# Expert weights of the third pair requested ahead of the first row gather, in a one-core encoder layer with a mixture of experts

## The reference, cut to what matters

```python
x = x + concat(A_out, B_out) @ w_out
h = rmsnorm(x, g_ffn)
# top-1 of 4 groups, then top-2 of the 8 experts inside the group
for e in range(32):
    gu  = h @ w_e_in[e]                        # 1024 x 512: gate | up
    act = silu(gu[:, :256]) * gu[:, 256:]
    out += gates[:, e:e+1] * (act @ w_e_out[e])   # 256 x 1024
y = rmsnorm(x + out, g_final)
```

## Time and profile before

| what | value |
|---|---|
| median of 3 runs | 601.9 us (601.87 to 603.3) |
| the profiled execution, its own time | 601.35 us |
| its span, first to last instruction | 599.6 us |
| mean granted TensorE clock | 0.972 |
| busy: PE, DVE, ACT, POOL | 545.6, 290.4, 166.0, 113.5 us |
| DMA queue q1 (SyncE): packets, MB | 39687, 139.63 |
| DMA queue q0 (GpSimd): packets, MB | 4464, 8.80 |

### The profile page before, as it was taken

How to read it: one execution, slowest core, us unless ns; L and a number is a source line. 1 busy time by engine, 2 the same in 40 slices (tenths; PEclk the granted TensorE clock), 3 DMA queues, 4 the chain that set the end, 5 groups by cost and what they waited for, 6 DMA issues and landing times.

```text
span 599.6 us, 7835 instructions
## 1 busy us (share of the span) xinstructions
PE 545.6 (91%) x3097; PEld 332.0 (55%) x3098; DVE 290.4 (48%) x496; ACT 166.0 (28%) x263; POOL 113.5 (19%) x181
## 2 busy tenths in 40 slices
PE   6999999999999898899999799999999778878993
PEld 5679999999765543444554674344443333333331
DVE  2862899998867546564455851211112110011147
ACT  4512123222766774652101111011010000000013
POOL 3100000312444240500100220221112210121003
PEclk9999999999999998899999779999999999889998
DMA  8805645301401500049743869999999999999995
GB/s 292 221 1 165 221 141 170 112 1 42 177 2 63 220 0 1 0 126 413 288 149 129 302 244 422 424 426 423 422 423 425 423 424 420 422 423 421 416 371 170
DMA packets 44188, 148.94 MB, mean 248 GB/s; under 512 B 7060, under 2 KB 23468, under 8 KB 35703
## 3 DMA queue, kind: packets, MB, share of 16 engines
q1 hardware_dynamic: 39687, 139.63, 60.1%
q0 software_dynamic: 4464, 8.80, 3.9%
HBM read 136.29 MB, written 19.59 MB: 260 GB/s over the span
## 4 chain that ended last, share of the span: by engine, by line
PE 64%; DMA 17%; DVE 8%; SPq 3%; ACT 3%; issue 3%; POOL 1%; DVEq 0%; POOLq 0%
PE ps L956 17%; PE ps L1361 10%; PE ps L1181 8%; DMA big<-in_w_expert_out 7%; PE ps L1386 6%; DMA low<-in_w_expert_out 5%; PE ps L921 3%; PE ps L1066 2%; SPq L599 2%; PE ps L1063 2%; DMA cw<-in_cache_v 2%; PE ps L1342 2%; DMA y_dram<-cw,low 1%; PE ps L1025 1%; PE ps L1087 1%
## 5 line engine op out<-in xcount | busy, mean ns | idle before, releaser
L1791 DVE SCALAR_TENSOR_TENSOR big<-low,cwt,big 128x590 f32<-128x590 f32 x120 | 95.1, 848 | 0.4
L2168 DVE TENSOR_TENSOR low<-low,ps 128x256 f32<-128x256 f32 x16 | 6.7, 421 | 173.7 <-ACT low L1653 173.7
L1361 PE MATMUL ps<-big,low 128*64 128x512 f32 x320 | 85.0, 593 | 3.0 <-issue 2.2
L956 PE MATMUL ps<-cw_r 128*128 128x288 f32 x256 | 73.0, 295 | 0.0
L956 PE MATMUL ps<-low_r,cw_r 128*128 128x288 f32 x256 | 72.8, 294 | 0.0
L956 PE MATMUL ps<-cw_r,big_r 128*128 128x288 f32 x256 | 72.7, 294 | 0.0
L1181 PE MATMUL ps<-cw,low 128*128 128x512 f32 x128 | 56.7, 594 | 0.2 <-DVE low L1913 0.2
L1386 PE MATMUL ps<-big,low 128*64 128x512 f32 x176 | 41.9, 618 | 14.3 <-DMA big<-in_w_expert_out 9.2
L1361 PEld LDWEIGHTS ps<-big,low 128*64 128x64 f32 x320 | 29.8, 137 | 45.4 <-issue 45.3
L956 PEld LDWEIGHTS ps<-cw_r 128*128 128x128 f32 x256 | 47.4, 188 | 0.4 <-issue 0.4
L956 PEld LDWEIGHTS ps<-cw_r,big_r 128*128 128x128 f32 x256 | 47.2, 188 | 0.0
(11 more groups left out here) (281 smaller groups left out, 851.7 us busy)
## 6 DMA issues: line engine op xcount, KB each, us to landing
big<-in_w_expert_in SPq DMA_DIRECT2D x16, 2048.0 KB, 20.7
big<-in_w_expert_out SPq DMA_DIRECT2D x22, 1024.0 KB, 24.8
low<-in_w_expert_in SPq DMA_DIRECT2D x8, 2048.0 KB, 26.5
big<-in_w_in SPq DMA_DIRECT2D x20, 512.0 KB, 5.5
low<-in_w_expert_out SPq DMA_DIRECT2D x10, 1024.0 KB, 31.3
cw<-in_w_expert_in SPq DMA_DIRECT2D x4, 2048.0 KB, 28.3
big<-in_w_expert_in SPq DMA_DIRECT2D x6, 1024.0 KB, 35.5
y_dram<-big SPq DMA_DIRECT2D x9, 512.0 KB, 5.1
```

The source lines that it names most:

```text
L956: return pe.matmul(ps[:, proj_bank(j) + half, 0:HALF], w[:, k, :], h[:, k, cols], start=first, stop=last, skip_group_check=True)
L1361: mm = pe.matmul(ps[TILE * half:TILE * half + TILE, gu_bank(g), :], xt[:, k, TILE * half:TILE * half + TILE], wi[(2 * g + half) % WI_SLOTS ...
L1791: ins = dve.scalar_tensor_tensor(conv[:, i, :], u[:, i, j:j + CW], cwt[:, i, j:j + 1], conv[:, i, :], ALU.mult, ALU.add)
```

## The change

It has six parts.
1. SyncE no longer waits for gather 0 ahead of expert 5's load (it waits for the stores of the normed rows, which its slot holds), nor for the gates' table ahead of pair 2's down weights (but for the logits' last reads, `gsub_ready` 3).
2. DVE writes the row numbers as integers from the start (`rows_of`), so that the casts on GpSimd ahead of every gather and scatter go, with their semaphores. The last pair's row numbers are kept once more as floats (`last_rows`).
3. ACT takes each pair's gates from the table itself; GpSimd's copies of them (L801) go.
4. PE computes the gate table behind pair 0's gate-and-up instead of ahead of it; DVE's `gates_in` moves behind pair 0's `copy_act_t`.
5. Pair 0's transposed rows are copied half by DVE, half by ACT.
6. `WARM` goes from 12 to 8.

```diff
-WARM = 12
+WARM = 8
...
             sp.wait_ge(logit_done, NC)
             sp.wait_ge(h2_stored[0], 16 * 3)
-            sp.wait_ge(gathered[0], 16)
+            sp.wait_ge(h2_stored[1], 16 * 2)
             load_wi(5)
-            sp.wait_ge(h2_stored[1], 16 * 2)
-            sp.wait_ge(tab_ready, 2)
+            sp.wait_ge(gsub_ready, 3)
             load_wo(2)
...
-                pool.tensor_copy(idx[b], tab[:, g, 0:1]).then_inc(idx_ready, 1)
-                pool.wait_ge(idx_ready, g + 1)
                 pool.indirect_dma_start(
                     out=xg[b], out_offset=None, in_=h2_dram,
-                    in_offset=bass.IndirectOffsetOnAxis(ap=idx[b].bitcast(U32), axis=0),
+                    in_offset=bass.IndirectOffsetOnAxis(ap=rows_of[:, g, 0:1].bitcast(U32), axis=0),
...
                 for k in range(KD):
+                    if g == 0 and k == KD // 2:
+                        pe.wait_ge(h2t_ready, NC + 1)
...
             turn(0)
-            gate_table()
             for g in range(PAIRS - 1):
                 gate_up(g)
+                if g == 0:
+                    gate_table()
                 turn(g + 1)
...
-                act.wait_ge(gat_ready, g + 1)
+                if g == 0:
+                    act.wait_ge(tab_ready, 2)
...
-                               ACT.Copy, scale=gat[b]).then_inc(yg_ready, 1)
+                               ACT.Copy, scale=tab[:, g, 2:3]).then_inc(yg_ready, 1)
+            act.wait_ge(xg_turned, 1)
+            act.copy(xt[:, KD // 2:KD], ps[:, 1, :].rearrange("p (k t) -> p k t", t=P)).then_inc(h2t_ready, 1)
...
-            dve.tensor_scalar(tab[:, :, 0:2], sums2, BIGF, None, ALU.add).then_inc(tab_ready, 1)
+            dve.tensor_scalar(rows_of, sums2, BIGF, None, ALU.add).then_inc(tab_ready, 1)
+            link(dve.tensor_scalar(last_rows, sums2[:, PAIRS - 1, 0:1], BIGF, None, ALU.add))
...
+                if g == 0:
+                    dve.tensor_copy(xt[:, 0:KD // 2], ps[:, 0, :].rearrange("p (k t) -> p k t", t=P)).then_inc(xt_ready, 1)
+                    return
...
             copy_xt(0)
-            gates_in()
             further_tiles()
             for g in range(PAIRS - 1):
                 gate_times_up(g)
                 copy_act_t(g)
+                if g == 0:
+                    gates_in()
                 copy_xt(g + 1)
```

More of the change, by code:

```diff
@@ L190, in build @@
         tab = rest[:, 1536:1536 + 4 * PAIRS].rearrange("p (g f) -> p g f", f=4)
-        idx = [rest[:, 1600 + b:1601 + b].bitcast(I32) for b in range(ROW_BUFS)]
-        oidx = [rest[:, 1604 + b:1605 + b].bitcast(I32) for b in range(ROW_BUFS)]
-        gat = [rest[:, 1608 + b:1609 + b] for b in range(ROW_BUFS)]
+        rows_of = tab[:, :, 0:2].bitcast(I32)
+        last_rows = rest[:, 1600:1601]
+        more_in = rest[:, 1604:1605].bitcast(I32)
+        more_out = rest[:, 1605:1606].bitcast(I32)
         more_tab = rest[0:TILE, 1612:1616]
@@ L228, in build @@
         entry = [late(640 + 128 * c, 128).rearrange("p (k f e) -> p k f e", k=2, f=2) for c in range(NC)]
-        gentry = [rest[:, 1024 + 64 * c:1088 + 64 * c].rearrange("p (k e) -> p k e", k=2) for c in range(NC)]
+        gentry = [late(640 + 64 * c, 64).rearrange("p (k e) -> p k e", k=2) for c in range(NC)]
         gex = late(1280, NC * NG)
@@ L352, in build @@
         pool_passed = sem("pool_passed")
-        idx_ready = sem("idx_ready")
-        gat_ready = sem("gat_ready")
-        oidx_ready = sem("oidx_ready")
         gathered = [sem(f"gathered{b}") for b in range(ROW_BUFS)]
@@ L806, in scatter @@
                     pool.wait_ge(scattered[b], g // ROW_BUFS * 16)
-                pool.tensor_copy(oidx[b], tab[:, g, 1:2]).then_inc(oidx_ready, 1)
-                pool.wait_ge(oidx_ready, g + 1)
                 pool.wait_ge(yg_ready, g + 1)
@@ L812, in scatter @@
                 pool.indirect_dma_start(
-                    out=y_dram, out_offset=bass.IndirectOffsetOnAxis(ap=oidx[b].bitcast(U32), axis=0),
+                    out=y_dram, out_offset=bass.IndirectOffsetOnAxis(ap=rows_of[:, g, 1:2].bitcast(U32), axis=0),
                     in_=yg[b], in_offset=None, bounds_check=2 * COLS - 1,
                     oob_is_err=False).then_inc(scattered[b], 16)
[L817 to L821, removed]
+            for g in range(LAG):
                 gather(g)
@@ L825, in _ @@
                 gather(g)
-                gates(g - LAG + ROW_BUFS)
                 scatter(g - LAG)
             for g in range(PAIRS - LAG, PAIRS - 1):
-                if g + ROW_BUFS < PAIRS:
-                    gates(g + ROW_BUFS)
                 if g == PAIRS - 3:
@@ L839, in more @@
                 pool.sem_inc(pool_passed, 1)
-                pool.tensor_copy(idx[0][0:TILE], more_tab[:, 0:1]).then_inc(more_idx, 1)
-                pool.tensor_copy(oidx[0][0:TILE], more_tab[:, 1:2]).then_inc(more_idx, 1)
+                pool.tensor_copy(more_in[0:TILE], more_tab[:, 0:1]).then_inc(more_idx, 1)
+                pool.tensor_copy(more_out[0:TILE], more_tab[:, 1:2]).then_inc(more_idx, 1)
                 pool.wait_ge(more_idx, n * 2 + 2)
@@ L845, in more @@
                     out=xg[0][0:TILE], out_offset=None, in_=h2_dram,
-                    in_offset=bass.IndirectOffsetOnAxis(ap=idx[0][0:TILE].bitcast(U32), axis=0),
+                    in_offset=bass.IndirectOffsetOnAxis(ap=more_in[0:TILE].bitcast(U32), axis=0),
                     bounds_check=COLS - 1, oob_is_err=False).then_inc(more_gathered, 16)
@@ L850, in more @@
                 pool.indirect_dma_start(
-                    out=y_dram, out_offset=bass.IndirectOffsetOnAxis(ap=oidx[0][0:TILE].bitcast(U32), axis=0),
+                    out=y_dram, out_offset=bass.IndirectOffsetOnAxis(ap=more_out[0:TILE].bitcast(U32), axis=0),
                     in_=yg[0][0:TILE], in_offset=None, bounds_check=2 * COLS - 1,
@@ L1340, in turn @@
                     pe.wait_ge(xt_ready, g)
+                if g == 1:
+                    pe.wait_ge(h2t_ready, NC + 1)
                 for k in range(KD):
@@ L2196, in _ @@
             dve.wait_ge(y_done, PAIRS - 2)
-            dve.tensor_tensor(pick15, tokens, tab[:, PAIRS - 1, 0:1].broadcast_to([P, COLS]), ALU.is_equal).then_inc(places_ready, 1)
+            dve.tensor_tensor(pick15, tokens, last_rows.broadcast_to([P, COLS]), ALU.is_equal).then_inc(places_ready, 1)
             gate_times_up(PAIRS - 1)
```

6 lines of the change are left out of this document (removed).

## The result

| | before | changed |
|---|---|---|
| median | 602.01 us (8 runs, 599.78 to 604.81) | 606.32 us (8 runs, 604.37 to 608.84) |
| profiled execution, span | 599.6 us | 602.6 us |
| mean granted clock | 0.972 | 0.97 |

The ratio is 1.0078, 95% interval 1.0056 to 1.01: the change makes the kernel about 4.7 us slower. The forecast was 607.0, with 601.2 to 609.8 as its range. Every ratio in this text is to runs of the kernel before that were taken beside the kernel in question; their median lay between 601.5 and 603.2 us, so the ratios are to be compared and not the medians. The medians of some variants include single slow executions of 802 to 3,062 us, which the ratios leave out.

The account below looks back on a forecast made before the run. The end was taken as bound by weight bytes at 423 GB/s. 0 before 344 us, +5.0 at expert 7's load and 0 after took 601.35 to 606.4; the new median was put at 607.0, range 601.2 to 609.8.

Parts of the forecast that it names:

- The end is set by bytes behind expert 7's load: From 362.4 us the DMA streams at 423 GB/s, so a later start of expert 7's load moves the end equally.
- The early loads: SyncE issues expert 5's load at about 340.0 instead of 350.42, pair 2's down weights at about 345.1 instead of 353.89.
- Gather 0: Pair 0's gather, issued at about 346.5 and sharing the DMA with 4.2 MB of weights, lands at 354.2 instead of 350.4.
- twin: Gather 2, issued at 355.07 amid expert weights, taken as model for gather 0: last packet about 7.7 us after issue.
- turns of many descriptors: Skill's rule that engines serve queues a packet at a time, which would barely delay one small gather.
- PE's low clock: PE at 1.2 GHz when gather 0 lands: transposes 1.8 us, pair 0's gate-and-up 7.1 plus 1.7, ending at 365.8.
- The load into an empty queue: Expert 7's load starts slowly behind an empty queue: +1.9 us, so in effect at 367.7 against 362.7.
- Other edits at nothing: Casts and gate copies removed from GpSimd, and the extra copy of the last row numbers on DVE: 0.
- The unslowed gather: Rival: gather 0 lands at 349.9 despite the weight stream; median 601.2 to 602.3; chance 0.17.
- head start: Rival: the weight stream starts 6 to 7 us earlier and ends so, 595 to 596; chance 0.04.
- caught up: Rival: PE's slack absorbs part of the delay in the stretch to 562 us; say 603; chance 0.05.
- full price: Rival: gather 0 lands at 356.7 and the clock loss is 2.8 instead of 1.7; 610.6; chance 0.12.

Follow-up runs that it names:

- half release in the kernel before: Kernel before, experts 7 and 8 loaded in two halves, the first asked for when pair 0 has used k = 0 to 3: 601.81 us, ratio 0.9984.
- the order undone: Changed kernel, but SyncE waits for gather 0 again ahead of expert 5's load: 601.73 us, ratio 1.0013.
- order alone: Kernel before with only SyncE's two requests (expert 5, pair 2's down weights) moved ahead of gather 0: 611.27 us, ratio 1.0132.
- expert 5 early: Changed kernel, only expert 5's load stays ahead of gather 0; pair 2's down weights wait for the gather: 605.12 us, ratio 1.0054.
- 34 filler products: Changed kernel with WARM = 34 instead of 8, to keep PE busy until gather 0 lands: 604.84 us, ratio 1.0046.
- changed kernel with half release: Changed kernel, experts 7 and 8 loaded in two halves, the first asked for when pair 0 has used k = 0 to 3: 606.72 us, ratio 1.0059.
- packets of 4 KB: Changed kernel, expert 5's load cut in four slices and each down matrix in two, giving 4 KB pieces: 607.47 us, ratio 1.006.

## Why the prediction was right, point by point

- *The end is set by bytes behind expert 7's load.* Shown: the last scatter moved by 5.0 for 5.6 in the changed kernel, and like it in five others. With a full queue an earlier request brought nothing (half release in the kernel before). The reservation is the second hole above: the tie is to PE's later releases too.
- *The early loads.* Forecast at +8.8 and +13.9, measured at +9.3 and +14.2.
- *Gather 0.* Forecast issue +15.3, landing 7.7 us later, from gather 2 as a twin. Measured +15.6 and 8.1; with the order undone 3.5. The removal of the cast saved 0.1 to 0.3 in most kernels and nothing in this execution. The twin was well chosen: gather 2 too had the down weights asked for just ahead of it, and 4.1 us without a packet. That turns of many descriptors would "barely delay" a small gather did not follow in the prediction, which never said what such a turn of the weights takes; here 4.4 us passed before the first packet.
- *PE's low clock.* Forecast transposes 1.8, handover 0.9, gate-and-up 7.1 + 1.7. Measured 1.97, 0.88 and 8.46. Of the clock terms in other kernels 2.7 and 2.8 occurred as well (order alone, expert 5 early), the upper bound that was kept. The reason given, that the clock would simply stay low as the dense stretch is broken, is not what happened: it had come up by 351 to 352 in the changed kernel (0.95), with PE idle since 347.9, fell to 0.50 at 352 to 353, just ahead of the transposes, and came back from 358 on (0.64) [windows above]. The numbers came out, the way to them did not; that is luck. The 34 filler products show that the term itself was real, 2.3 us.
- *The load into an empty queue.* Forecast +1.9 against a backlog of 2.0, so +5.0 for an issue at +34.6. The issue came at +35.1, so the sum would be 5.5; measured 5.0. The slow start was set a little too dear: at 131 GB/s from 364.4 to 366.4 it loses 1.4 us of stream against 422, and 391 GB/s over the next 3.6 us another 0.3. The issue's half microsecond too early and this one too much cancel, which is luck too.
- *Other edits at nothing.* The order undone gives 1.0013 (0.9988 to 1.0039): right for all of them together, within that interval. The gate table was put at 0 under the cover of the weight queue and at +1.4 without it; the changed kernel with half release, where the queue does run dry before pair 1's end, shows 1.2 (13.8 us of PE's work against 12.6).
- *The unslowed gather*, the strongest rival, is refuted by the 8.1, the *head start* by the hole, *caught up* by the last scatter, which moved with the load. Of the *full price* neither half came here (8.1 us and not 10.2; a clock loss of 1.4 and not 2.8), though 2.8 did in other kernels. That an unslowed gather beside early loads would bring nothing was not tested: with the order undone the gather is fast, but the loads are not early.

## What to carry to other kernels

Ahead of a byte-bound stretch, ask what lets the *next* request go, not how early the present ones can be made: a load that is moved forward earned nothing here, as the one behind it still waited for a slot. A small gather on which everything waits should meet an empty queue, or one whose work ends as it arrives. A split of the slot's release cost nothing measurable where the queue was full, and brought some 2.7 us where it ran dry just ahead of the release; and a filler that keeps the clock up must last until the work comes.

## What the runs showed of the hardware

- A gather of 0.2 MB takes 3.5 to 3.6 us alone, 5.1 to 5.8 behind the request of expert 5, and 8.0 to 9.2 with the down weights asked for as well (7.1 with packets of 4 KB). Its first packet moves after 1.9 to 2.0, 2.5 to 2.6 and 4.4 to 4.6 us, the last with packets of 4 KB too.
- A filler that ended 2.5 us too soon was worse than one that ended 5.2 too soon (transposes and gate-and-up 11.05 us against 10.43): what counts is where the low stretch falls.
- Executions of one unchanged front part differ by up to 4.4 us at expert 4's load (329.1 to 333.5), with low-clock stretches in some executions that others lack. In a comparison of single profiles that is as large as the effect, so the comparison was made from a common mark.
